# Decay gaps of an SSD chunk as one subtraction clipped on ScalarE, and the products with C on GpSimd

## The reference

```python
def step(state, inp):                       # one chunk
    acum = jnp.cumsum(dtc * a, axis=1)      # running decay exponent, 128 tokens x 16 heads
    diff = acum[:, :, None] - acum[:, None]
    seg = jnp.exp(jnp.where(mask, diff, -jnp.inf))
    xdt = xc * dtc[..., None]
    scores = jnp.einsum('bihn,bjhn->bijh', cc, bc) * seg
    y_intra = jnp.einsum('bijh,bjhp->bihp', scores, xdt)
    y_inter = jnp.einsum('bihn,bhpn->bihp', cc * jnp.exp(acum)[..., None], state)
    a_last = acum[:, -1]
    w = jnp.exp(a_last[:, None] - acum)[..., None]
    state = state * jnp.exp(a_last)[..., None, None] + jnp.einsum('bjhn,bjhp->bhpn', bc * w, xdt)
    return state, y_intra + y_inter
```

## Time and profile before

| | us |
|---|---|
| median of three runs | 2242.17 |
| their range | 2240.55 to 2242.7 |
| the profiled execution, its own time | 2242.34 |
| its span | 2240.5 |
| TensorE busy | 2169.5 |
| VectorE busy | 1243.9 |
| ScalarE busy | 724.8 |
| GpSimd busy | 52.3 |

### The profile page before, as it was taken

The page is one execution under the profiler, slowest core; times in us unless marked ns, Lnnn a source line. Parts: engine busy times, 40 slices in busy tenths (PEclk is TensorE's granted clock), DMA queues, the critical chain, the costliest instruction groups (busy, mean ns, idle before and its releaser), DMA issues.

```text
span 2240.5 us, 28163 instructions
## 1 busy us (share of the span) xinstructions
PE 2169.5 (97%) x10212; PEld 1778.6 (79%) x10212; DVE 1243.9 (56%) x2008; ACT 724.8 (32%) x998; POOL 52.3 (2%) x94
## 2 busy tenths in 40 slices
PE   6999999999999989999999999999997999999998
PEld 5888888787878778888888888888755778888886
DVE  6534446597547987435446544445578535534444
ACT  4222223333325453222223222223365653222222
POOL 0000000000000000000000000000002210000000
PEclk8999999999999999999999999999898999999999
DMA  4334333321134313545453333332210013333322
GB/s 144 94 98 105 100 90 98 94 67 49 48 94 122 85 57 104 113 112 113 108 115 97 103 95 93 103 94 87 83 50 10 1 38 89 99 95 102 94 82 69
DMA packets 361965, 195.64 MB, mean 87 GB/s; under 512 B 13619, under 2 KB 356790, under 8 KB 361878
## 3 DMA queue, kind: packets, MB, share of 16 engines
q1 hardware_dynamic: 359238, 184.73, 29.0%
q0 software_dynamic: 2640, 9.77, 2.7%
HBM read 191.55 MB, written 2.79 MB: 87 GB/s over the span
## 4 chain that ended last, share of the span: by engine, by line
PE 88%; DVE 8%; issue 1%; ACT 1%; SPq 1%; DMA 1%; DVEq 0%; ACTq 0%
PE ps L1390 25%; PE ps L1392 25%; PE ps L1391 25%; PE ps L1772 2%; PE ps L1794 1%; PE ps L1512 1%; PE ps L1409 1%; PE ps L1410 1%; PE ps L1411 1%; DVE w_lo L743 1%; DVE index_scores L1280 1%; PE ps L1763 1%; DVE stat L1263 1%; DVE index_scores L1265 1%; PE ps L1440 0%
## 5 line engine op out<-in xcount | busy, mean ns | idle before, releaser
L448 ACT ACTIVATE w_hi<-w_raw 128x1024 fp32r<-128x1024 f32 x351 | 372.0, 1060 | 1096.0 <-PE ps L1392 1048.6
L1390 PE MATMUL ps<-h_hi,w_hi 128*128 128x512 f32 x1704 | 668.2, 392 | 0.6 <-issue 0.6
L1391 PE MATMUL ps<-h_lo,w_hi 128*128 128x512 f32 x1704 | 665.2, 390 | 0.0
L1392 PE MATMUL ps<-h_hi,w_lo 128*128 128x512 f32 x1704 | 664.9, 390 | 0.0
L743 DVE TENSOR_TENSOR w_lo<-w_raw,w_hi 128x1024 fp32r<-128x1024 f32 x351 | 429.2, 1223 | 291.8 <-ACT w_hi L448 291.7
L1390 PEld LDWEIGHTS ps<-h_hi,w_hi 128*128 128x128 f32 x1704 | 321.2, 189 | 68.2 <-issue 1.3
L1392 PEld LDWEIGHTS ps<-h_hi,w_lo 128*128 128x128 f32 x1704 | 321.2, 189 | 67.4
L1391 PEld LDWEIGHTS ps<-h_lo,w_hi 128*128 128x128 f32 x1704 | 321.2, 189 | 66.0
L1390 PE MATMUL ps<-act_hi,w_hi 128*128 128x512 f32 x704 | 273.9, 389 | 0.0
L1391 PE MATMUL ps<-act_lo,w_hi 128*128 128x512 f32 x704 | 273.9, 389 | 0.0
L1392 PE MATMUL ps<-act_hi,w_lo 128*128 128x512 f32 x704 | 273.9, 389 | 0.0
(11 more groups left out here) (273 smaller groups left out, 2046.3 us busy)
## 6 DMA issues: line engine op xcount, KB each, us to landing
w_raw<-in_ffn_w_gate SPq DMA_DIRECT2D x88, 512.0 KB, 3.8
w_raw<-in_ffn_w_up SPq DMA_DIRECT2D x88, 512.0 KB, 3.8
w_raw<-in_ffn_w_down SPq DMA_DIRECT2D x64, 512.0 KB, 4.0
w_raw<-in_hy_w_in SPq DMA_DIRECT2D x44, 512.0 KB, 3.7
w_raw<-in_ffn_w_down SPq DMA_DIRECT2D x32, 384.0 KB, 3.5
w_raw<-in_hy_w_out SPq DMA_DIRECT2D x16, 512.0 KB, 4.2
acum_rows<-acum_scratch POOLq DMA_DIRECT2D x4, 1024.0 KB, 10.6
bias_rows<-line_scratch POOLq DMA_DIRECT2D x8, 512.0 KB, 6.8
```

Of the source, the lines that this page charges most:

```text
L448: act.activation(w_hi[:, s, :], w_raw[:, s, :], ACT.Copy).then_inc(hi_ready, 1)
L1390: pe.matmul(ps[:, bank, :], wh, rh[:, k, :], start=k == 0, stop=False)
L1391: pe.matmul(ps[:, bank, :], wh, rl[:, k, :], start=False, stop=False)
L1392: mm = pe.matmul(ps[:, bank, :], wl, rh[:, k, :], start=False, stop=k == nk - 1)
```

## The change

VectorE's 16 instructions per chunk (subtract and clip at 0, one per head) become one tensor_tensor of 128x2048 that computes own - row, unclipped and with its sign turned. ScalarE clips it from below at 0 with a Relu, and then takes the exponential with scale -1. The two products with C leave VectorE and stand on GpSimd, in the list that also issues the row loads.

```diff
@@ gpsimd
-                for c in range(TT):
-                    if c >= 2:
-                        pool.wait_ge(s_y, c - 1)
+                def chunk_rows(c):
                     pool.dma_start(acum_rows[:, c % 2, :, :], ...).then_inc(s_acb[c % 2], 16)
+                def from_start(c):
+                    pool.wait_ge(s_ea, 2 * c + 2)
+                    hg = SH // SG
+                    for g in range(SG):
+                        ce = acum_rows[:, c % 2, g * hg:(g + 1) * hg, :]
+                        pool.tensor_tensor(ce, ce, xbc[:, 10 + g:11 + g, c * P:(c + 1) * P].to_broadcast([P, hg, P]), ALU.mult).then_inc(s_C, 1)
+                chunk_rows(0)
+                chunk_rows(1)
+                pool.wait_ge(s_silu, XT)
+                from_start(0)
+                from_start(1)
+                for c in range(2, TT):
+                    pool.wait_ge(s_y, c - 1)
+                    chunk_rows(c)
+                    from_start(c)
@@ scalar, decays(c)
                     act.wait_ge(s_D, c + 1)
-                    act.activation(ssd_attn[:, c % 2, :, :], ssd_attn[:, c % 2, :, :], ACT.Exp).then_inc(s_pexp, 1)
+                    act.activation(ssd_attn[:, c % 2, :, :], ssd_attn[:, c % 2, :, :], ACT.Relu).then_inc(s_relu, 1)
+                    act.wait_ge(s_relu, c + 1)
+                    act.activation(ssd_attn[:, c % 2, :, :], ssd_attn[:, c % 2, :, :], ACT.Exp, scale=-1.0).then_inc(s_pexp, 1)
@@ vector, gaps(c)
-                    for h in range(SH):
-                        ins = dve.tensor_scalar(ssd_attn[:, c % 2, h, :], acum_chunk[:, h, :], acum_tok[:, c, h:h + 1], 0.0, ALU.subtract, ALU.min)
-                    ins.then_inc(s_D, 1)
+                    dve.tensor_tensor(ssd_attn[:, c % 2, :, :], acum_tok[:, c, :].rearrange("p (h o) -> p h o", o=1).to_broadcast([P, SH, P]),
+                                      acum_chunk, ALU.subtract).then_inc(s_D, 1)
@@ vector: from_start(c) and its two calls are gone
-                def from_start(c):
-                    dve.wait_ge(s_ea, 2 * c + 2)
...
-                        dve.tensor_tensor(ce, ce, xbc[:, 10 + g:11 + g, c * P:(c + 1) * P].to_broadcast([P, hg, P]), ALU.mult).then_inc(s_C, 1)
...
                 dve.wait_ge(s_silu, XT)
-                from_start(0)
...
-                        from_start(c + 1)
```

More of the change, by code:

```diff
@@ L263, in build_program @@
         s_cbm, s_tr, s_trB, s_Bev, s_xdt, s_xdtw = (sem(n) for n in ("s_cbm", "s_tr", "s_trB", "s_Bev", "s_xdt", "s_xdtw"))
-        s_y, s_yev, s_st, s_S1, s_S2, s_gate = (sem(n) for n in ("s_y", "s_yev", "s_st", "s_S1", "s_S2", "s_gate"))
+        s_relu, s_y, s_yev, s_st, s_S1, s_S2, s_gate = (sem(n) for n in ("s_relu", "s_y", "s_yev", "s_st", "s_S1", "s_S2", "s_gate"))
         l_landed, l_mm, l_ev, l_scr, t_landed = (sem(n) for n in ("l_landed", "l_mm", "l_ev", "l_scr", "t_landed"))
@@ L1068, in gaps @@
                     acum_chunk = acum_rows[:, c % 2, :, :]
-                    for h in range(SH):
-                        ins = dve.tensor_scalar(ssd_attn[:, c % 2, h, :], acum_chunk[:, h, :], acum_tok[:, c, h:h + 1], 0.0, ALU.subtract, ALU.min)
-                    ins.then_inc(s_D, 1)
+                    dve.tensor_tensor(ssd_attn[:, c % 2, :, :], acum_tok[:, c, :].rearrange("p (h o) -> p h o", o=1).to_broadcast([P, SH, P]),
+                                      acum_chunk, ALU.subtract).then_inc(s_D, 1)
                     dve.tensor_tensor(wtok[:, c % 2, 0, :], acum_chunk[:, :, P - 1], acum_tok[:, c, :], ALU.subtract).then_inc(s_wd, 1)
-                def from_start(c):
-                    dve.wait_ge(s_ea, 2 * c + 2)
-                    for g in range(SG):
-                        ce = acum_rows[:, c % 2, g * hg:(g + 1) * hg, :]
-                        dve.tensor_tensor(ce, ce, xbc[:, 10 + g:11 + g, c * P:(c + 1) * P].to_broadcast([P, hg, P]), ALU.mult).then_inc(s_C, 1)
                 def z_tile(m):
```

## The result

| | before | changed |
|---|---|---|
| median, us (five runs each) | 2242.17 | 2253.01 |
| range, us | 2240.55 to 2243.29 | 2252.42 to 2255.53 |
| profiled execution, its own time | 2242.34 | 2254.19 |
| its span | 2240.5 | 2252.4 |

A forecast was written before the change was run, and what follows sets the result against it. It took VectorE to bound the stage at 732 to 812 us, with row-load slack of only 6.1 and 4.1 us. Late loads +13.9 and the tail +0.1 gave +14.0 us on 2242.34, so 2256, range 2247 to 2266.

The forecast's parts named there:

- The order on GpSimd: Row loads of chunks 2 and 3 wait behind the previous chunk's products; gaps(2) +7.1 us, gaps(3) +13.9.
- ScalarE's chain of 7.4 us: In decays, from the gaps' end to s_ea: Relu, table load and exponentials in a row, 7.4 us against 4.0.
- GpSimd's products: Each 128x1024 product with C on GpSimd taken as 2.24 us, lower bound 1.12, upper bound 3.36.
- Each waits for the other: GpSimd's products and VectorE's instructions with two SBUF inputs: whichever starts later waits; without it +8.5 us, not +14.
- The landing: Row loads of chunks 2 and 3: each lands 10.4 us after its issue.
- Loads that take less: Rival on the row loads: 9 us instead of 10.4 as less else moves, total +11.2; no separate chance given.
- The start: Chunk 0 to gaps(1): Relu in decays(0) makes the last silu 0.9 to 1.0 us later; gaps(1) at 742.5 against 742.23.
- The tail: From gaps(3) to the first final update of the last chunk: 22.6 us against 22.5 before, +0.1.
- VectorE's saving: Gaps and from_start on VectorE: 3.2 of 18.9 us relieved per chunk, but it drops out of the cycle.
- The faster rival: VectorE's relief carries through if chunk 2's load is issued before 750.6: -4.6 us if products do not block; chance 0.03.
- TensorE's clock: Nothing added for TensorE's z units, even if its clock drops in two new holes of about 5 us, chunks 2 and 3.
- the prediction's own cases: Blocking products, +10 to +18: 0.55; cheaper or not blocking, +4 to +10: 0.25; dearer 0.14; relief 0.03; cancelling changes 0.03.

The follow-up runs named there:

- memset run: The changed kernel with GpSimd's two products replaced by memsets of the same 128x1024 halves, leaving out the product with C; 2241.77 us, one run.

## Why the prediction was right, step by step

The forecast was +14 us, 2256, range 2247 to 2266; measured +10.8 by the medians, 2253.01, and +11.85 by the two profiled executions. The case that it named the likeliest came about.

- **The order on GpSimd decides: right, and shown.** Loads at 757.20 and 782.11, forecast "about 758 and 783". Moving them alone takes away the whole loss (2242.78).
- **ScalarE's chain of 7.4 us: right to the tenth.** A Relu of 128x2048 takes 1.90 us, like an exponential, and the table load is paid behind the wait. Taking the table load out of it gave about 4 us back.
- **GpSimd's products: right in size, low by 0.1.** A pair takes 5.73 us including the wait for VectorE's `w_lo`. Alone, a product of 128x1024 takes 2.38 us (the shortest of the eight, one that met nobody), where I took 2.24; the upper bound was far off.
- **Each waits for the other: right.** The first product starts at 751.52 and holds `w_lo`, which takes 2.58 us instead of 1.22; `w_lo` then holds the second product, and that holds `xdtw` (1.42 instead of 1.23). The memset run shows that it is not the writing.
- **The landing: the term that was mis-sized.** I took 10.4 us from the two rows of before; the loads of chunks 2 and 3 landed after 9.5 and 9.25 (from the issue to VectorE's start). That is 2.0 of the 2.4 us by which `gaps(3)` came earlier than forecast (791.36 against 793.8). "Loads that take less" stood among the rivals, with 9 us and +11.2, and came about beside the forecast. Its reason, less other traffic, is not borne out: in the 10 us after the issue at 744.65 before, the DMA moved 107 GB/s, hardly more than the load's own 1 MB, and in the 9 us after 757.20 in the changed kernel 152 GB/s, and that load was the faster one.
- **The start: 0.7 us too late.** `gaps(1)` was forecast for 742.5 and came at 741.82. I let the last silu come 0.9 us later; it came 0.3 later (final silu at 732.11, before 731.82). I had counted the Relu at `decays(0)` but not that ScalarE reaches it earlier, at 712.39 and not 713.07, since the shorter `gaps(0)` had drawn the convolution forward. Without this and the landing the steps give 14.0 - 0.7 - 2.0 = 11.3 us, against the 11.64 by which the final update moved.
- **The tail: right.** From `gaps(3)` to the final update it is 22.7 us, forecast 22.6.
- **VectorE's saving is swallowed: right.** The subtraction takes 2.28 us as worked out. The products back on VectorE (+3.6 by the medians) and the loads moved first (+0.1) show that the saving appears in neither.
- **The faster rival: its condition was right.** It needed loads issued before 750.6. With the loads first they are, and the time is still no better. Its -4.6 was for products that do not hold VectorE up, and these do; ScalarE's chain also meets VectorE through `w_hi`, as its text had it. Only with that chain in the other order does a gain come, of 3.6 us.
- **TensorE's clock: no part in it.** The clock did drop at the two new holes: TensorE stood idle for 1.9 and 2.1 us, until VectorE's `xdtw` of chunks 1 and 2 was done, and within a microsecond of its going on the granted clock fell to 0.50 (1.2 GHz) for some 3.4 us, from about 759.4 and 783.3; before, it was 1.00 from 720 to 800. The chunk's matmuls in these stretches were over by 765.8 and 790.7, ahead of `gaps(2)` and `gaps(3)`, and VectorE had no new wait for TensorE.
- **The chances: off by 0.01.** By the prediction's own cases slower is 0.55 + 0.20 + 0.14 = 0.89 and same 0.08, where it says 0.90 and 0.07.

What stays open: what sets the landing time, which for the loads of chunks 2 and 3 went from 9.2 to 11.0 us between the kernels; what the order on ScalarE would be worth by itself; and whether it is the reading alone that holds VectorE up.

## What to carry to other kernels

An engine that issues transfers has an order: an operation put into its list delays every transfer behind it by its own wait too, here by 12.6 us for 5.7 us of work, and the slack of those transfers (6.1 and 4.1 us) is the first number to look up. Before work is moved off the busiest engine, follow what it waits for: here the moved work waited for the longest chain of another engine, and putting that chain's urgent member first took the 11 us off the changed kernel, while the move itself is worth 2 at the most. An instruction that needs another function table pays for the load behind its wait, here 1.3 us each time, unless a small instruction with that table stands ahead of it.

## What the runs showed of the hardware

- GpSimd multiplies two float32 tensors of 128x1024 in 2.38 us, VectorE in 1.22. With one float32 input GpSimd would take 1.12 us for that size, an estimate from the slope of rows 7, so the second input about doubles the time.
- A VectorE instruction with two SBUF tensors and a GpSimd instruction that reads SBUF run one after the other: 1.22 us became 2.58 beside a product, and stayed 1.23 beside a memset.
- VectorE's instruction with one input in PSUM (`xdt`, 1.21 us at 755.60) ran beside a GpSimd product without a change.
- The same 1 MB row load landed between 9.2 and 11.0 us after its issue when it was issued alone, with no reason that the traces show.
- One execution of 11 of one kernel took 4096 us instead of 2241. Nothing in the runs says why.
